# Half of the hybrid mixer's out-projection as a seventh chain among the other six, with another table for their order

## The reference

```python
def hybrid_mixer(h, w_in, conv_w, a_log, dt_bias, gdn_norm, sb_q_norm, sb_k_norm, w_out):
    proj = h @ w_in
    gq, gk, gv, gate, ga, gb, sq, sk, sv = _split(proj, HYB_SPLITS)
    ...                      # convolution, SiLU, l2 norm of q and k
    o_a = gated_delta_rule(qa, ka, va, g, beta)          # 4 heads of 128
    o_a = rms_norm(o_a, gdn_norm) * silu(gate)
    o_b = stick_breaking_attention(qb, kb, vb)           # 8 heads of 64
    return concatenate([o_a, o_b]) @ w_out               # 1024 x 1024

# in the block
x = x + gt_m * hybrid_mixer(h, ...)
h = rms_norm(x, norm_ffn[l]) * (1 + sc_f) + sh_f
x = x + gt_f * swiglu(h, ...)
```

## Time and profile before

| | |
|---|---|
| median of 3 runs | 2846.86 us (2842.31 to 2851.11) |
| profiled execution | 2848.74 us, its span 2846.9 us |
| PE busy | 2753.4 us (97%) |
| DVE, ACT, POOL busy | 1428.4 (50%), 962.5 (34%), 556.2 us (20%) |
| chain that ended last | PE 87%, DVE 7%, ACT 4% |
| mean granted clock | 0.992 |

### The profile page before, as it was taken

How to read it: one execution, slowest core, us unless ns; L and a number is a source line. 1 busy time by engine, 2 the same in 40 slices (tenths; PEclk the granted TensorE clock), 3 DMA queues, 4 the chain that set the end, 5 groups by cost and what they waited for, 6 DMA issues and landing times.

```text
span 2846.9 us, 31909 instructions
## 1 busy us (share of the span) xinstructions
PE 2753.4 (97%) x13258; PEld 2192.1 (77%) x13258; DVE 1428.4 (50%) x2078; ACT 962.5 (34%) x1264; POOL 556.2 (20%) x422
## 2 busy tenths in 40 slices
PE   7999989999999999999999999999999998999998
PEld 4877667888887787788888877778888875788886
DVE  6746647566554343372222455655345465544453
ACT  3445444222233232252222333432222344332222
POOL 3564311100112212221001200022022100121121
PEclk9999999999999999999999999999999999999999
DMA  6322113455332222223632322122322321222322
GB/s 246 126 90 104 45 39 147 185 192 212 124 112 81 85 93 74 93 76 108 171 118 71 119 87 82 67 89 86 108 96 80 113 63 63 81 93 86 112 77 71
DMA packets 51088, 296.28 MB, mean 104 GB/s; under 512 B 6617, under 2 KB 6745, under 8 KB 25088
## 3 DMA queue, kind: packets, MB, share of 16 engines
q1 hardware_dynamic: 44912, 276.58, 27.5%
q0 software_dynamic: 4736, 15.34, 2.0%
q10 hardware_dynamic: 1296, 2.32, 0.2%
HBM read 283.46 MB, written 8.65 MB: 103 GB/s over the span
## 4 chain that ended last, share of the span: by engine, by line
PE 87%; DVE 7%; ACT 4%; issue 1%; DMA 1%; POOL 0%; SPq 0%; DVEq 0%; ACTq 0%
PE ps L218 86%; DVE wlo L211 1%; PE ps L1336 1%; ACT whi L200 1%; DVE F L2483 1%; DVE hl L306 1%; ACT F L1353 0%; DMA F<-in_ada 0%; DVE F L418 0%; ACT hh L290 0%; DMA raw<-in_gdn 0%; DVE hl L422 0%; DVE Rf L2483 0%; DVE ada L466 0%; DVE F L833 0%
## 5 line engine op out<-in xcount | busy, mean ns | idle before, releaser
L218 PE MATMUL ps<-hh,whi 128*128 128x512 f32 x2088 | 826.9, 396 | 10.0 <-DVE hl L306 4.5
L218 PE MATMUL ps<-hl,whi 128*128 128x512 f32 x2088 | 814.8, 390 | 0.0
L218 PE MATMUL ps<-hh,wlo 128*128 128x512 f32 x2088 | 813.9, 390 | 0.0
L211 DVE TENSOR_TENSOR wlo<-raw,whi 128x2048 fp32r<-128x2048 f32 (+2 forms) x235 | 499.6, 2127 | 506.9 <-ACT whi L200 504.6
L200 ACT ACTIVATE whi<-raw 128x2048 fp32r<-128x2048 f32 (+2 forms) x235 | 409.7, 1743 | 745.7 <-PE ps L218 740.8
L218 PE MATMUL ps<-R,whi 128*128 128x512 f32 x2080 | 653.2, 392 | 7.7 <-DVE wlo L211 2.8
L218 PEld LDWEIGHTS ps<-hh,whi 128*128 128x128 f32 x2088 | 392.7, 188 | 102.0 <-issue 7.5
L218 PEld LDWEIGHTS ps<-R,whi 128*128 128x128 f32 x2080 | 390.6, 188 | 95.2 <-issue 7.0
L218 PEld LDWEIGHTS ps<-hl,whi 128*128 128x128 f32 x2088 | 392.5, 188 | 83.5
L218 PEld LDWEIGHTS ps<-hh,wlo 128*128 128x128 f32 x2088 | 392.9, 188 | 80.6 <-issue 2.2
L218 PE MATMUL ps<-R,wlo 128*128 128x512 f32 x1040 | 404.9, 389 | 0.0
(11 more groups left out here) (345 smaller groups left out, 2504.7 us busy)
## 6 DMA issues: line engine op xcount, KB each, us to landing
F<-in_ada SPq DMA_DIRECT2D x32, 1024.0 KB, 4.9
raw<-in_fs0in SPq DMA_DIRECT2D x22, 1024.0 KB, 5.5
raw<-in_fs1in SPq DMA_DIRECT2D x22, 1024.0 KB, 4.7
raw<-in_fc0in SPq DMA_DIRECT2D x22, 1024.0 KB, 4.7
raw<-in_fc1in SPq DMA_DIRECT2D x22, 1024.0 KB, 4.7
Rf<-in_ada0h SPq DMA_DIRECT2D x24, 512.0 KB, 3.5
raw<-in_fs0out SPq DMA_DIRECT2D x16, 704.0 KB, 4.3
raw<-in_fs1out SPq DMA_DIRECT2D x16, 704.0 KB, 4.2
```

The costliest lines, as they stand in the source:

```text
L211: e.tensor_tensor(m.wlo[n % 2][:, 0:size], m.raw[m.slot[n]][:, 0:size], m.whi[n % 2][:, 0:size].bitcast(F32), SUB).then_inc(*s.up("wlo", n))
L218: return e.matmul(out, l, r, start=start, stop=stop, skip_group_check=True)
```

## The change

The out-projection is cut over k into two halves. The first half, over the tiles k = 0, 4, 1, 5 (`OUT_ROWS`), becomes a seventh chain `o` of 34 steps in the mixer: two slabs `hybo0` of 512 outputs, each 4 output tiles of 4 pieces, a piece being one `mm3`. Every four pieces DVE adds the bank to x. The second half, over k = 6, 2, 3, 7 (slabs `hybo1`), follows the mixer (`pe_hyb_last`), the first slab with k outermost into four banks, the second tile by tile into four others. DVE does it in the manner of the even mixer's `dve_out_last`, with the shift sums ahead of the residuals; ACT uses `act_out_last`. The table of steps is another one: 558 steps, the 34 of `o` at places 398 to 557, and the other six chains in a different merge too. The assertion on `needs` while the table is read is dropped; the semaphores are as they were.

```diff
-KC = {..., "dlv": 4, "eveno0": 4, ...}
+KC = {..., "dlv": 4, "hybo0": 4, "hybo1": 4, "eveno0": 4, ...}
...
-CHAINS = {"d": "delta0", "e": "delta1", "s": "stick", "h": "heads", "a": "ada", "g": "gates"}
+OUT_ROWS = ((0, 4, 1, 5), (6, 2, 3, 7))
+def out_steps():
+    ready = (("out", 0), ("out", 1), ("sb", 1), ("sb", 3))
+    for j in range(2):
+        for n in range(16):
+            beside = ("act:1.9", "dve:2.1")[n] if n < 2 else "" if n % 4 else "dve:0.7"
+            yield step("pe:0.7", ("slab", "hybo0", j) if n == 0 else None, beside, ready)
+        yield step("dve:0.7", ("free",))
+CHAINS = {"o": "out", "d": "delta0", ...}
 ORDER = """
-e h d e2 h3 d e4 h d e3 d h d e h2 d e h3 e2 h3
+e h o h e d o3 a o2 h d o d e h e2 o d a e d e h2 a o e h o e o h d2 o e h d2 e d h e h2 a e o
...
+    elif name == "hybo0":                                  # pe_dense_free
+        s.wait_ge("x", "hyb", "half", 4 * j + 3)
...
+def pe_out_chain(e, s, m):
+    for j in range(2):
+        slab = m.at["hybo0", j]
+        pe_dense_free(s, m, slab)
+        s.wait_ge("wlo", slab)
+        hi, lo = m.w(slab)
+        for c in range(4):
+            if c >= 2:
+                s.wait_ge("x", "hyb", "half", 4 * j + c - 2)
+            cut = slice(c * P, (c + 1) * P)
+            for i, k in enumerate(OUT_ROWS[0]):
+                hyb_out_ready(s, k)
+                t = mm3(e, m.ps[c % 2][:, :], hi[:, i, cut], lo[:, i, cut], *m.o(k), i == 0, i == 3)
...
+                yield
+        yield
+def dve_out_chain(e, s, m):
+    for j in range(2):
+        slab = m.at["hybo0", j]
+        for n in range(17):
+            if n == 1:
+                dve_slab(e, s, m, slab + 1)
+            elif n and n % 4 == 0:
+                c = n // 4 - 1
+                dve_residual(e, s, m, "hyb", slab, c, 4 * j + c, c % 2, GATE["hyb"], ("hyb", "half", 4 * j + c))
+            yield
+HYB_BANKS = (0, 1, 2, 3, 4, 7, 5, 6)
+def pe_hyb_last(e, s, m):
+    slab = m.at["hybo1", 0]
+    pe_dense_free(s, m, slab)
...
+    for i, k in enumerate(OUT_ROWS[1]):
+        hyb_out_ready(s, k)
+        for n in range(4):
+            if i == 0 and n == 2:
+                s.wait_ge("o_lo", "hyb", 2)
+            t = mm3(e, m.ps[HYB_BANKS[n]][:, :], ...)
...
+    for n in range(4):                                     # the second slab
+        for i, k in enumerate(OUT_ROWS[1]):
+            t = mm3(e, m.ps[HYB_BANKS[4 + n]][:, :], ...)
...
+def dve_hyb_last(e, s, m):
+    slabs = m.at["hybo1", 0], m.at["hybo1", 1]
+    dve_gain(e, s, m, MODULATED["hyb"])
+    dve_slab(e, s, m, slabs[1])
+    dve_shift_sums(e, s, m, "hyb", slabs[1] + 1)
+    for n in range(4):
+        dve_residual(e, s, m, "hyb", slabs[0], n, n, HYB_BANKS[n], GATE["hyb"], ("hyb", n))
+    dve_slab(e, s, m, slabs[1] + 1)
+    for n in range(4):
+        dve_x(e, s, m, "hyb", n)
+    for n in range(4, 8):
+        dve_residual(e, s, m, "hyb", slabs[1], n - 4, n, HYB_BANKS[n], GATE["hyb"], ("hyb", n))
+        dve_x(e, s, m, "hyb", n)
...
-    take("hybo", range(4))
+    take("hybo1", range(2))
...
-    pe_mix_out(e, s, m, "hyb", "hybo", hyb_ready(s, m))
+    pe_hyb_last(e, s, m)
-    act_mix_out(e, s, m, "hyb", "hybo")
+    act_out_last(e, s, m, "hyb", "hybo")
-    dve_mix_out(e, s, m, "hyb", "hybo")
+    dve_hyb_last(e, s, m)
-    sp_mix_out(e, s, m, "hybo")
+    for j in range(2):
+        sp_slab(e, s, m, m.at["hybo1", j] + 2)
```

More of the change, by code:

```diff
@@ L2261, in head_steps @@
         yield step(work)
-    yield step("act:0.6", None, "pool:1.5", needs=("modulation",) if h == 2 else ())
+    yield step("act:0.6", None, "pool:1.5", needs=("modulation",) if h == 2 else (), done=("out", h))
 GATE_STEPS = ("pe:5.6", "dve:0.7", "pe:0.6", "dve:0.6", "act:2.2", "dve:0.9", "pe:0.5", "dve:0.6", "act:0.9", "dve:0.3")
@@ L2343, in hybrid_order @@
     chains = {"delta0": list(delta_steps(0)), "delta1": list(delta_steps(1)), "heads": list(stick_head_steps()),
-              "stick": list(stick_steps()), "ada": list(ada_steps()), "gates": list(gate_steps())}
-    at, order, slabs, before, held, last, done = dict.fromkeys(chains, 0), [], [], {}, False, None, set()
+              "stick": list(stick_steps()), "ada": list(ada_steps()), "gates": list(gate_steps()), "out": list(out_steps())}
+    at, order, slabs, before, held, last = dict.fromkeys(chains, 0), [], [], {}, False, None
     for i in (CHAINS[word[0]] for word in ORDER.split() for _ in range(int(word[1:] or 1))):
-        _, mark, _, needs, finished = chains[i][at[i]]
-        assert all(n in done for n in needs), (i, at[i])
+        mark = chains[i][at[i]][1]
         if mark and mark[0] == "slab":
@@ new lines, in sp_out_chain @@
+def sp_out_chain(e, s, m):
+    for j in range(2):
+        sp_slab(e, s, m, m.at["hybo0", j] + 2)
+        yield from steps(17)
+HYB_BANKS = (0, 1, 2, 3, 4, 7, 5, 6)
+def pe_hyb_last(e, s, m):
+    slab = m.at["hybo1", 0]
+    pe_dense_free(s, m, slab)
+    s.wait_ge("wlo", slab)
+    hi, lo = m.w(slab)
+    for i, k in enumerate(OUT_ROWS[1]):
[3 more added lines that the diff above has]
+                s.wait_ge("o_lo", "hyb", 2)
+            t = mm3(e, m.ps[HYB_BANKS[n]][:, :], hi[:, i, n * P:(n + 1) * P], lo[:, i, n * P:(n + 1) * P], *m.o(k), i == 0, i == 3)
+            if i == 3:
+                t.then_inc(*s.up("tile", slab, n))
+    s.also("tile", slab, "all")
+    slab = m.at["hybo1", 1]
+    s.wait_ge("wlo", slab)
+    hi, lo = m.w(slab)
+    for n in range(4):
+        for i, k in enumerate(OUT_ROWS[1]):
+            t = mm3(e, m.ps[HYB_BANKS[4 + n]][:, :], hi[:, i, n * P:(n + 1) * P], lo[:, i, n * P:(n + 1) * P], *m.o(k), i == 0, i == 3)
+        t.then_inc(*s.up("tile", slab, n))
+    s.also("tile", slab, "all")
```

61 lines of the change are left out of this document (36 added, 25 removed).

## The result

The changed kernel takes 2818.81 us, median of 4 runs (2818.29 to 2819.25), against 2847.55 for the kernel before beside it: ratio 0.9896, 95% interval 0.9883 to 0.991. It is 1% faster. The profiled execution has a span of 2817.4 us, 29.5 less than before.

What follows compares the result with a forecast made beforehand. PE was taken as the bound in most of the mixer, with 24.8 us idle, and the out-projection as solid. Seam 12.6 shorter, 21.9 moved in, 18.5 filled or regained: 9.2 us shorter, 2838 us, range 2825 to 2851.

Steps and rivals of the forecast that it cites:

- R: In the mixer, PE idle time filled plus clock regained, offsetting the added matmuls: 18.5 us, between -1 and 30.
- the seam: From the end of the last head's sums to the feed-forward's third slab: 76.7 us before, 64.1 predicted, 12.6 shorter.
- the work moved: 96 of 192 out-projection matmuls go into the mixer, 21.9 us of PE, none added or dropped.
- T0: End of head 7's cumulative sums on PE, from which the steps behind the mixer are counted: 415.0 before.
- PE's new wait for the last residual: Behind the mixer, PE stands still until VectorE's last residual completes x: 5.5 us.
- lost cover: Behind the mixer, the moved 21.9 us had also covered VectorE's work, so 9.3 us are given back.
- The exchange of both: 21.9 us more PE work in the mixer against 12.6 us saved behind it: 9.3 us slower if nothing is filled.
- Early order: In the mixer before 300, only the six old chains' other order acts on 14.7 us idle: 6.5 us, bounds -5 and 13.
- Late idle filled: In the mixer from 300 to 415, out steps fill most of 10.0 us of PE idle: 8 us, bounds 4 and 10.
- The clock: In the mixer, half level at 318 to 326 regained: 4 us, bounds 0 and 7.
- Everything fits: Rival: mixer holes nearly vanish and the clock stays up, 18.7 us shorter, 2828 us; chance 0.14.
- The recurrences set the length: Rival: delta heads, not PE's time, set the mixer's length; nothing filled, 9.3 us slower, 2856 us; chance 0.12.

Runs made afterwards that it cites:

- e4_turns: The changed kernel with VectorE's residuals 4 to 7 placed between low parts 0 to 3 in the hybrid stage's last half: 2814.0 us, ratio 0.9876.
- e3_end: The changed kernel with all 34 out steps behind the last step of the six old chains, which keep the new order: 2838.7 us, ratio 0.9966.
- e1_table: The kernel before with the new order of its six old chains, no out steps, the old out-projection whole behind the mixer: 2827.3 us, ratio 0.9926.
- e9_ada_moved: The kernel before with only the 30 modulation steps at their new places, other five chains in the old order, no out steps: 2856.1 us, ratio 1.0023.
- e10_rest_moved: The kernel before with the other five chains in the new order, the 30 modulation steps at their old places, no out steps: 2852.4 us, ratio 1.0018.
- e5_chain: The changed kernel with the six old chains in the old order and the 34 out steps over the last 104 of 524 steps: 2851.5 us, ratio 1.001.

## Why the prediction was wrong, point by point

It failed at R, the time filled and regained in the mixer, and there first at the term for the new order; the seam and the work moved came out.

**The seam (12.6 shorter) was right**: 12.3 by the trace of the changed kernel. Its steps, as predicted and measured behind T0: roots done 4.3 and 4.1, products 5.7 and 5.7, copy of head 3 6.4 and 6.3, its low part 8.2 and 8.0, first slab landed 13.9 and 12.8, shift sums done 17.9 and 16.8, x complete 39.3 and 38.4, third slab 64.1 and 64.4. PE's new wait for the last residual was put at 5.5 and is 5.05. Half level followed behind it, as it might: the squares took 2.08 and 3.60, against 1.02 and 1.88 at full clock in e4_turns. Where I was off inside, it cancelled, which is luck: the slab landed 1.1 us sooner, residuals 4 to 7 came 3.25, 3.21 and 2.72 apart rather than 3.2, and the third slab started 1.2 us longer behind x than I had it. The reason given for the price, lost cover, was wrong (e3_end): it is paid for the cut over k, and 6.6 us came back with another order of turns on VectorE (e4_turns).

**The work moved (21.9) was right.** The exchange of both was put at 9.3 us against the change. e3_end against e1_table shows that sum without interleaving: 11.3 slower.

**R was the step that failed**: 18.5 with an upper bound of 30, measured 18.8 + 21.9 = 40.7. By its terms:

- *Early order, 6.5 (bound 13)*. All of the reordering, with no out steps, measured 21.5 (e1_table). I had priced it by the idle time alone, and thought of it as a side effect of the table. Of the 21.5, 16.0 come with the first 224 steps and 5.5 with the later ones, on the one way measured. Idle fell by 7.6 on balance (25.1 to 17.5). The rest, 13.9, is PE's busy time. About 2.3 of it is work that now stands behind the exponential. PE was busy 21.4 us at half level in 40 to 415 before and 9.2 in e1_table: 12.2 less, worth at most half of that, 6.1. At least 5.5 us more went from busy time at the same work; I take it for time in which a matmul's record was open and waited, but that is worked out by difference, and no run isolates it.
- *Late idle filled, 8 (bound 10)*. The out steps filled 19.2 of their 21.9 us (393.9 to 396.6). The bound was wrong in kind: I took the holes of the old order as all that there is to fill, but the new order leaves 17.5 us of idle, 13.7 of it late. Of the 17.5, 13.3 went, and the remaining 6 are half level (9.2 us busy to 0.6, at most 4.3) and time counted busy. In the old order the same steps filled 4.9, less than I said. My 8 was right for neither order.
- *The clock, 4 (bound 7)*. Before, 21.4 us of busy time stood at half level from 40 to T0 (in 90.0 to 96.9, 315.3 to 329.0 and 387.0 to 390.4), after 0.6: at most 10.4 us. I had looked at one stretch, the four windows of the earlier trace rows, and not at all of them.

So 40.7 is 20.9 of idle, at most 10.4 of clock, about 1.8 of sums that now stand behind T0, and at least 7.6 that left the busy time otherwise. What that last part is stays open, and so does how the order brings it. The bounds failed because I read them from a trace in which the order was the old one, term by term, as if terms that one table sets could be added. They can't: e9_ada_moved and e10_rest_moved cost 0.23 and 0.18% apart and give 0.74% together, and the out chain costs the mixer 17.0 us in one order and 2.6 in the other.

**The rivals.** "Everything fits" (0.14) was the nearest: the holes nearly vanish and the clock stays up, though its R of 28 was short as well. Its argument against was that the holes before 180 come before any output exists. True, but they went without anything being put in: 6.5 of the 11.5 us went when the modulation was moved, and with it GpSimd's work from beside VectorE's taps. The rows on which that could have been seen were in the trace of before: taps of 1600 and 1772 ns in the mean beside one of the same size at 749. "The recurrences set the length" is what e5_chain does in the old order, at three quarters of its price (17.0 of 21.9).

By the Trainium skill (TensorE: Matmul & The Clock Gate, section "HAM oscillation — how this bites in real kernels") a wait of this kind sends the array back to half rate and the burst after it pays. I had held this against the change. The trace agrees at the seam, where it cost 2.7 us on the squares. But it speaks for the change over the whole mixer, where the half level that went with the holes had cost up to 10.4.

## What to carry to other kernels

A new table for a hand-written order is a change of its own: price it apart from what it was made to hold, and give its bound by everything that the order can move (idle, time at half level, and operations that run at twice their best time), not by idle alone. Look in one group for the same operation at two durations: it shows that another engine is in the way where no wait names it. At the end of a stage, take what completes the input of the next stage before the work that merely follows from each piece; a turn that waits for another engine each time (1.31 us here) shows where.

## What the runs showed of the hardware

VectorE and GpSimd hold each other up far more than I had reckoned. In the kernel before, a tap of 128x511 takes 749 to 751 ns where no GpSimd instruction overlaps it and 2385 where GpSimd overlaps 2307 of those ns. In the rows looked at the later of two pays: GpSimd's 128x1024 product took 3.70 us at 64.08, begun behind VectorE's low part, and 1.90 at 118.88 and at 138.53, begun first, where VectorE's tap took 2.33 instead of 0.75 and its low part 3.80 instead of 2.29. This reached PE without one long wait of PE for GpSimd: 0.4 us in all in 40 to 180, while moving the modulation away took 6.5 us off PE's idle time there.
